# Five post-norm gain vectors travel through a row in DRAM instead of through TensorE

## What is computed

```python
# first block, per layer:
x = x + g1 * rms_norm(mixer(h), norm_g[layer, 1])   # mixer: gMLP (layer 0), sparse attention (layer 1)
x = x + g2 * rms_norm(ffn(h),   norm_g[layer, 3])   # ffn: square(relu(h @ ff_w_in)) @ ff_w_out
# second block:
x = x + gt1 * rmsnorm(token_mixers(h) @ w_out, g_post_mix)   # gated linear attention + short conv
x = x + gt2 * rmsnorm(conv_ffn(h), g_post_ffn)
# rms_norm(y, g) = y * rsqrt(mean(y*y) + eps) * g
# g1, g2, gt1, gt2 are parts of (silu(c) @ ada_w + ada_b): vectors of 1024, equal for all tokens
```

## Time and profile before

| what | value |
|---|---|
| median of 3 runs | 1009.01 us (1007.38, 1009.01, 1009.29) |
| profiled execution, its own time | 1008.37 us |
| its span in the profile | 1006.5 us |
| TensorE busy | 980.9 us, 97% of the span |
| VectorE busy | 800.8 us, 80% |
| ScalarE busy | 539.7 us, 54% |
| DMA, mean rate | 242 GB/s |

### The profile page before, as it was taken

How to read it: one execution, slowest core, us unless ns; L and a number is a source line. 1 busy time by engine, 2 the same in 40 slices (tenths; PEclk the granted TensorE clock), 3 DMA queues, 4 the chain that set the end, 5 groups by cost and what they waited for, 6 DMA issues and landing times.

```text
span 1006.5 us, 16927 instructions
## 1 busy us (share of the span) xinstructions
PE 980.9 (97%) x6900; PEld 864.0 (86%) x6901; DVE 800.8 (80%) x1208; ACT 539.7 (54%) x706; POOL 77.4 (8%) x80
## 2 busy tenths in 40 slices
PE   6999999999999999999999999999999999999997
PEld 3687799989987999886889999988998889999996
DVE  1449799858988978877978878872799799888896
ACT  4354554444446567765545454465765765454544
POOL 0000000000000000000630000000791000000000
PEclk9999999999999999999999999999999999999999
DMA  9999699969997997014998787725444386555511
GB/s 338 387 386 377 220 340 394 353 233 363 347 335 259 269 375 279 2 43 128 391 358 306 279 284 286 250 85 167 127 142 132 105 289 214 191 186 193 184 43 42
DMA packets 130332, 243.60 MB, mean 242 GB/s; under 512 B 6586, under 2 KB 95311, under 8 KB 124111
## 3 DMA queue, kind: packets, MB, share of 16 engines
q1 hardware_dynamic: 125616, 238.77, 67.1%
q10 hardware_dynamic: 4639, 3.76, 1.4%
HBM read 239.37 MB, written 1.05 MB: 239 GB/s over the span
## 4 chain that ended last, share of the span: by engine, by line
PE 77%; DVE 8%; POOL 4%; ACT 3%; DMA 3%; issue 2%; SPq 2%; POOLq 0%; DVEq 0%; ACTq 0%
PE bank L2050 25%; PE bank L1982 12%; PE bank L1984 11%; PE bank L1983 11%; DMA raw<-in_a_w_in_dram 3%; PE bank L2062 2%; PE bank L2335 1%; DVE wlo L1202 1%; PE bank L2361 1%; PE bank L1876 1%; ACT t L778 1%; POOL eb L2717 1%; SPq L657 1%; PE bank L2373 1%; DVE hcat L1347 1%
## 5 line engine op out<-in xcount | busy, mean ns | idle before, releaser
L1202 DVE TENSOR_TENSOR wlo<-raw,whi 128x2048 fp32r<-128x2048 f32 x143 | 327.2, 2294 | 49.6 <-ACT whi L727 48.5
L727 ACT ACTIVATE whi<-raw 128x2048 fp32r<-128x2048 f32 x144 | 274.2, 1905 | 138.8 <-PE bank L2050 69.9
L1982 PE MATMUL bank<-hcat,whi 128*128 128x256 f32 x1096 | 308.9, 282 | 0.7 <-DVE wlo L1202 0.7
L1983 PE MATMUL bank<-hcat,whi 128*128 128x256 f32 x1096 | 306.8, 280 | 0.0
L1984 PE MATMUL bank<-hcat,wlo 128*128 128x256 f32 x1096 | 306.8, 280 | 0.0
L1982 PEld LDWEIGHTS bank<-hcat,whi 128*128 128x128 f32 x1096 | 206.0, 188 | 7.3 <-issue 3.0
L1984 PEld LDWEIGHTS bank<-hcat,wlo 128*128 128x128 f32 x1096 | 208.8, 191 | 0.0
L1983 PEld LDWEIGHTS bank<-hcat,whi 128*128 128x128 f32 x1096 | 206.0, 188 | 1.4
L1829 DVE SCALAR_TENSOR_TENSOR cvt<-ut,vec,cvt 128x189 f32<-128x189 f32 (+2 forms) x176 | 68.2, 429 | 19.3 <-ACT cvt L1165 16.8
L2050 PE MATMUL bank<-whi,fhi 128*128 128x512 f32 x240 | 74.7, 392 | 0.0
L2050 PE MATMUL bank<-wlo,fhi 128*128 128x512 f32 x240 | 74.0, 389 | 0.0
(11 more groups left out here) (432 smaller groups left out, 1644.8 us busy)
## 6 DMA issues: line engine op xcount, KB each, us to landing
raw<-in_ada_w_dram SPq DMA_DIRECT2D x40, 1024.0 KB, 8.5
raw<-in_ff_w_in_dram SPq DMA_DIRECT2D x32, 1024.0 KB, 7.9
raw<-in_ff_w_out_dram SPq DMA_DIRECT2D x32, 1024.0 KB, 7.5
raw<-in_w_ada_dram SPq DMA_DIRECT2D x24, 1024.0 KB, 5.9
raw<-in_w_up_dram SPq DMA_DIRECT2D x22, 1024.0 KB, 5.1
raw<-in_w_in_dram SPq DMA_DIRECT2D x12, 1024.0 KB, 5.5
raw<-in_w_down_dram SPq DMA_DIRECT2D x11, 1024.0 KB, 4.9
raw<-in_ada_w_dram SPq DMA_DIRECT2D x16, 512.0 KB, 12.1
```

The source lines that it names most:

```text
L727: act.activation(whi[:, m % SPL, 0:w], raw[:, pl.nm[m] % RAW, 0:w], ACT.Copy).then_inc(s_hi, 1)
L1202: dve.tensor_tensor(wlo[:, m % SPL, 0:w], raw[:, pl.nm[m] % RAW, 0:w], whi[:, m % SPL, 0:w], ALU.subtract).then_inc(s_lo, 1)
L1982: pe.matmul(dst, wh[:, kt, n], ah[:, kt, :], start=kt == 0, stop=False)
L1983: pe.matmul(dst, wh[:, kt, n], al[:, kt, :], start=False, stop=False)
```

## The change

In the five stages after `U_GMLP` the vector goes another way. SP writes `coef[:, c, :]` to a row of an internal DRAM tensor, `gain_rows` (`gain_to_row`, a transfer of 1024 single elements of 4 bytes, since neighbours in DRAM lie in different partitions), and later reads the row into all 128 partitions of `gain` (`gain_to_all`, 128 x 4 KB). Both stand in SP's stream of weight loads, each ahead of a named load: the write ahead of chunk loads `M_FF+25`, `M_BO[0]`, `M_SB[0]` or `M_UP[4]`, the read ahead of `M_FF+31`, `M_FF[1]`, `M_UP[0]` or `M_UP[6]`. The write waits until the modulation vector is ready (`s_mod`), the read until the row is written, until x has been updated by the stage before, and in two stages for one semaphore more. VectorE waits for the read (`s_gall`) ahead of its first `times_gain`. The diagonals, the products of ones and the copies go, in these five stages.

```diff
+    GAIN_OF = {U_FF0: (G0B, G_N3), U_ATT: (G1A, G_N5), U_FF1: (G1B, G_N7), U_GLA: (G2A, G_N10), U_FF2: (G2B, G_N12)}
+    gain_rows = nc.dram_tensor("gain_rows", (5, D), F32, kind="Internal").ap()
...
+            def gain_to_row(u):
+                b, c = GAIN_OF[u]
+                sp.wait_ge(s_mod, mods_done(b))
+                sp.dma_start(gain_rows[u - 1].rearrange("(k p) -> p k", p=P), coef[:, c, :], allow_slow_non_contiguous=True).then_inc(s_grow, 16)
+
+            def gain_to_all(u):
+                sp.wait_ge(s_grow, 16 * u)
+                sp.wait_ge(s_x, 4 * u)
+                if u == U_ATT:
+                    sp.wait_ge(s_T, NH)
+                if u == U_GLA:
+                    sp.wait_ge(s_ms4, 2)
+                sp.dma_start(gain[:, :], gain_rows[u - 1:u].broadcast_to([P, D])).then_inc(s_gall, 16)
+
+            row_at, all_at = {}, {}
+            if has("ffn0"):
+                row_at[pl.nm[M_FF[0] + 25]], all_at[pl.nm[M_FF[0] + 31]] = U_FF0, U_FF0
+            if has("attn"):
+                row_at[pl.nm[M_BO[0]]], all_at[pl.nm[M_FF[1]]] = U_ATT, U_ATT
+            if has("ffn1"):
+                row_at[pl.nm[M_FF[1] + 25]], all_at[pl.nm[M_FF[1] + 31]] = U_FF1, U_FF1
+            if has("gla"):
+                row_at[pl.nm[M_SB[0]]], all_at[pl.nm[M_UP[0]]] = U_GLA, U_GLA
+            if has("ffn2"):
+                row_at[pl.nm[M_UP[4]]], all_at[pl.nm[M_UP[6]]] = U_FF2, U_FF2
+
             for n in range(NN):
+                if n in row_at:
+                    gain_to_row(row_at[n])
+                if n in all_at:
+                    gain_to_all(all_at[n])
...
                     dve.wait_ge(s_sqy, 4 * u + i + 1)
-                    if i < 2:
-                        dve.wait_ge(s_gain, 2 * u + i + 1)
+                    if i < 2 and u == 0:
+                        dve.wait_ge(s_gain, i + 1)
+                    elif i == 0:
+                        dve.wait_ge(s_gall, 16 * u)
...
-                    if c == 12:
-                        if f == 1 and has("gla"):
-
-                            dve.wait_ge(s_cT, 4)
-                        gain_diag(u, gain_of)
...
-                gain_diag(U_ATT, G_N5)
                 splits(M_BO[2] + 1)
...
-                    if c >= 13:
-
-                        pe.wait_ge(s_mid, u0 + c)
-                        gain_row(u, c - 13)
...
                 def gains():
                     pe.wait_ge(s_msr, 2)
-                    gain_row(U_GLA, 0)
-                    gain_row(U_GLA, 1)
                     pe.wait_ge(s_gs, 2)
```

More of the change, by code:

```diff
@@ L521, in build @@
     s_diag, s_gmm, s_gain = sem("gain_diagonal"), sem("gain_rows_multiplied"), sem("gain_rows_ready")
+    s_grow, s_gall = sem("gain_row_in_dram"), sem("gain_in_all_partitions")
     s_v, s_root = sem("half_of_the_squares"), sem("roots_ready")
@@ L869, in ffn @@
                     epi(c)
-                    if c >= 14:
-                        gain_row(u, c - 14)
                     splits(m0 + min(2 * c + 4, 33))
@@ L1018, in _ @@
                 ada_row(S1B)
-                gain_row(U_ATT, 0)
                 splits(M_BO[3] + 2)
-                gain_row(U_ATT, 1)
                 end_of_stage(U_ATT, M_BO[3])
@@ L1179, in _ @@
                 use_roots()
-                gain_row(U_FF2, 0)
-                gain_row(U_FF2, 1)
                 for tt in range(2):
@@ L1771, in _ @@
                 fill(8)
-                gain_diag(U_GLA, G_N10)
                 dve.wait_ge(s_cvh, 1)
@@ L1855, in _ @@
                     conv_epi(c)
-                    if c == CF - 3:
-                        gain_diag(U_FF2, G_N12)
                 update_x(U_FF2)
@@ L1943, in dummies @@
             def dummies(e):
-                pe.wait_ge(s_gain, 2 * e)
+                pe.wait_ge(s_gain, 2)
                 keep_warm(WARM_BOUNDARY, 6)
@@ L2108, in ffn @@
                 for c in range(15):
-                    if c == 14:
-                        pe.wait_ge(s_gain, 2 * u + 1)
                     ff_in(c + 1)
@@ L2428, in _ @@
                 x_transposes(4, 0)
-                pe.wait_ge(s_gain, 8)
                 pe.wait_ge(s_h, 8 * 6)
@@ L2626, in _ @@
                         up(M_GA[c + 1], 4 + (c + 1) % 2)
[L2627 to L2632, removed]
                     down(c)
```

## The result

The changed kernel takes 1011.71 us (median of 14 runs, 1009.10 to 1014.00), against 1008.38 for the kernel before (14 runs, 1006.85 to 1010.56). The ratio is 1.0032, with an interval of 1.0023 to 1.0042: slower by 3.3 us, where 1006.2 had been forecast. Its profiled execution is one of the quicker ones (1010.22, span 1008.5).

What follows compares the result with a forecast made beforehand. TensorE was taken to bound the kernel (77% of the chain), with other engines meeting it at stage ends; 0.49 + 0.90 + 0.70 + 0.66 + 0.10 = 2.85 us saved, from 1009.01 to 1006.2, range 1004.4 to 1009.9.

Steps and rivals of the forecast that it cites:

- FF0: At this stage's end, `whi` and VectorE's run behind it come earlier without the gain copy: 0.49 us saved, bounds 0.49 and 0.90.
- attention: At this stage's end, the last head pair's gating starts earlier, moving the next weights' transfer: 0.70 us saved, bounds 0 and 0.90.
- FF1: At this stage's end, `flo` is done early enough that TensorE gains all of the removed products' time: 0.90 us saved.
- linear attention: At this stage's last tile, TensorE starts earlier until it meets VectorE's `wlo`: 0.66 us saved, bounds 0.6 to 0.9.
- FF2: At this stage's last tile, VectorE's `clo` leaves TensorE little to gain: 0.10 us saved, bounds 0.06 to 0.2.
- the price of the writes: Row writes, tightest ahead of the attention's output weights: 0.6 to 3.0 us each, costing 0 to 0.65, 0 in the sum.
- the loads behind it in the same queue: In the weights' queue, a write delays the loads behind it by its own time, taken as 3.0 us.
- The slower rival: A write much dearer than any row holds up the attention's output weights, from 7.2 us delay: 1011.0 and above; chance 0.12.
- The first sign of being wrong: SP or a weight load appears before `whi` with more wait than now behind a write; no size given.
- the rival of half the gain: The attention's read delays FFN weights, or writes cost 0.65, or FF0 or FF1 loads are late: 1006.8 to 1008.1; chance 0.20.
- the prediction's rival of 0.05: In the attention, shifted work may move TensorE's half-clock dip, giving or taking 1 to 2 us; chance 0.05.
- The Trainium skill's rule: For the row writes: transfers below 512 bytes miss line rate and do a read-modify-write, so packets might cost twice, 1009.8; chance 0.07.

Runs made afterwards that it cites:

- e1: The changed kernel with only the attention's row write moved, from ahead of the output weights to ahead of the third modulation load behind them; 1005.86 us.
- e4: The changed kernel with the attention's row written at about the same time but from ScalarE's DMA queue; 1011.03 us, ratio 1.0031 to the kernel before.
- p4: e1 plus an unread write of 4 KB as 128 pieces of 32 bytes, ahead of the attention's output weights; 1006.16 us.
- p1: e1 plus an unread write of 512 pieces of 4 bytes side by side, ahead of the attention's output weights; 1006.33 us.
- p3: e1 plus a load of 1024 pieces of 4 bytes into SBUF that nobody reads, ahead of the attention's output weights; 1005.96 us.
- p6: e1 plus an unread write of 1024 pieces of 4 bytes, 16 bytes apart, ahead of the attention's output weights; 1004.77 us.

## Why the prediction was wrong

The five terms can be read from when the first transposes of x of the next stage start (for FF2: when VectorE's last addition to x starts). Each number is how much a stage became longer against before:

| stage | predicted | the change | e1 |
|---|---|---|---|
| FF0 | -0.49 | -0.52 | +0.10 |
| attention | -0.70 | +4.08 | -1.81 |
| FF1 | -0.90 | -0.90 | -0.89 |
| linear attention | -0.66 | -0.53 | -0.54 |
| FF2 | -0.10 | -0.21 | -0.20 |

**The gains were right.** FF0: TensorE now waits 0.43 for `flo`, whose VectorE run starts 0.51 earlier, at 285.97 (286.48 before):

```profile
285.97 2.29 DVE L1227 TENSOR_TENSOR wlo<-raw,whi 128x2048 fp32r<-128x2048 f32 x1 [0.58 <-ACT whi L760]
...
297.07 1.06 PE L1916 MATMUL bank<-acc_wide,one 128*32 128x512 f32 x8 [0.43 <-DVE flo L1531]
```

FF1 gave its full 0.90. In the linear attention the last tile starts 0.3 later than the spacing of the matmuls ahead of it would let it, in FF2 0.59, as forecast behind `wlo` and `clo`:

```profile
798.66 0.62 PE L2068 MATMUL bank<-whi,hcat 128*128 128x512 f32 x2
799.43 0.47 PE L2080 MATMUL bank<-whi,hcat 128*128 128x512 f32 x1
...
995.82 0.50 PE L2080 MATMUL bank<-whi,chi 128*128 128x512 f32 x1 [0.59 <-DVE clo L1871]
```

In the attention, from the head pair's last small matmuls to the transposes, before took 473.44 - 451.92 = 21.52, the change 21.03, e1 20.91: 0.49 and 0.61 of the 0.70. The next weights' issue came 0.7 earlier in that count (5.5 in place of 6.2) and behind the read, as forecast. With 0.52, 0.61, 0.90, 0.53 and 0.20 the sum is 2.76 against the 2.85 of the prediction; e1's median is 2.45 below before. e1's row differs from these in FF0 and the attention for a reason told at the end.

**The step that failed is the price of the writes.** This term of the sum was put at 0, with 0.65 as the most that it could cost; moving the attention's write alone gave 5.85 between the medians (e1), and TensorE's wait behind it is 3.77. The text took 0, "since the 4-byte packets are nearer to the tiny ones of the 9 ns row", and 3.0 us as the dearer end. The packets were as short as forecast, about 13 ns. But a packet's duration was the wrong row to price a write by: the loads beside and behind it ran at 14 to 110 GB/s, and 10.7 us of transfer were missing, 3.6 times the upper end. The path was wrong too: the text lets the write delay "the loads behind it in the same queue", but the load issued ahead of it came 7.9 later, and from another queue (e4) the write cost as much. The slower rival named the place (the output weights of the attention) and the point from which it decides, a delay of 7.2 us; the weights came 8.9 late. Its reason, dearer packets, was not the right one. The first sign of being wrong that the text names is the one that came: a weight load ahead of `whi`, waited for behind a write (7.99). Nor was the rival of half the gain: loads that are late in FF0 (ScalarE waits 8.04 for one at 260.70) cost little, and the read never stood in the way.

**What the 4.08 is made of.** The starts of the same matmul in both profiles, subtracted, show where the attention loses. The change comes into it 0.52 ahead. By 356 it is 0.10 ahead: from 340 to 350 it starts 90 matmuls and before 94, at a granted clock of 1.00, and why is open. Behind the wait of 3.77 it is 3.74 late. The matmuls directly behind that wait run at a low clock (0.51 from 388 to 390) until 391.5, and then it is 5.08 late; by 398.44, with a wait of 0.26, 5.69. From 432 to 436 it is before whose clock falls, and the change wins 1.51 back (below, the same eight matmuls before and after). At the end, with the gain, it is 3.57 late, and 0.52 + 3.57 is the 4.08, but for rounding.

```profile
434.41 1.71 PE L2335 MATMUL bank<-kc,qT 64*128 64x144 f32 x8
...
439.20 0.97 PE L2346 MATMUL bank<-kc,qT 64*128 64x144 f32 x8
```

So the dip of the clock, the prediction's rival of 0.05, moved with the wait and in these two profiles nearly cancels. Between the medians it may not: the profiled executions differ by 1.85 us, the medians by 3.33. The mean granted clock of the change's 14 executions is 0.9959 (0.993 to 0.999), of 25 of before, run beside e1, 0.9973 (0.996 to 0.999); 0.0014 of 1008 us is 1.4 us, an estimate of what the low clock adds. That the long wait is what brings it would fit, and no run separates the two.

The Trainium skill's rule that was weighed (page "DMA: Bandwidth & Descriptors", section "Specifications": below 512 bytes a transfer is short of line rate, with a read-modify-write) pointed the right way, and the size alone doesn't carry it. 32-byte pieces missed 0.4 us here, and 4-byte pieces 16 to 512 bytes apart 1.8 to 2.9, against 10.7 side by side. That a read-modify-write is what makes neighbours collide would fit; no run here shows what the memory does inside.

## What to carry to other kernels

A column written to a row in DRAM as single elements was cheap in packets here and dear in what it did to the loads beside it for about 10 us, from either of the two queues tried. So place it where no load is due, as e1 does (for 5.85 us), or try pieces of 32 bytes (0.4 us missed in p4) if the reader can use that order without a stride; no run here has such a reader. Price a transfer of a new kind by the rate of its neighbours, not by the duration of its packets, and put a wide upper end on a kind that no row shows.

## What was not expected of the hardware

In eight of the twelve profiles TensorE's granted clock fell once to its lower level, 1.2 GHz, in the middle of its work, at a place that differs; p1 has no such dip, p3 and p6 have two, and e4 has three, one of them twice as long. Before (first row below, 432 to 436, after small matmuls), the change (388 to 392, from the end of TensorE's wait of 3.77 on) and e1 (124 to 128, behind waits of 0.95 and 0.71 at a stage's start) each have one, shown as 0.57 over 4 us:

```profile
432.00:436.00 4.00, 4.00 (x24) 3.28 (x25) 2.70 (x7) 2.51 (x7) 0.00 (x0) 0.57 0.00 0
```

```profile
388.00:392.00 4.00, 3.50 (x18) 3.50 (x19) 2.72 (x3) 3.97 (x5) 0.00 (x0) 0.57 1.01 417
```

```profile
124.00:128.00 4.00, 3.93 (x20) 3.96 (x21) 3.98 (x15) 4.00 (x7) 0.00 (x0) 0.57 1.05 361
```

4 x 0.43 = 1.7 us of the full clock are lost in each. The dip falls into FF0 in e1 and into the attention in before and in the change. So e1's FF0 is 0.6 worse than the change's, and its attention better by more than its term: of the 1.81, 0.61 is the gain and 1.50 before's dip from 432 to 436, which e1 has not, less 0.30 that e1 loses earlier. e4's three low stretches lose 6.8 us in all, 3.4 of them from 386 to 394, where its wait of 4.45 ends, and its profile is 2.4 us longer than the change's. A difference of one or two us between two single profiles is no more than this.
